# The last tile's gates made in the pass before its own and kept in DRAM (hybrid MLA / sparse attention / PEER step)

## The chip, the cores and the metric

One core of one Trainium2 chip. The time is that of one launch on the device in microseconds (us), from the program's start to its end. The kernel before was run three times: 1798.29 us in the median, 1796.89 and 1798.40 at the ends.

## What is computed

One step of a streaming encoder layer for 512 prompt rows, 32 sample rows and 16 meta rows of 1024 columns, all in float32. Cut to what this case touches:

```
h = RMSNorm(x)
cq, ckv, kpe, bq, bk, bv, iq, iw, ik, ga, gb = split(h @ w_in)
o_a = latent attention(cq, ckv, kpe);  o_b = sparse attention(bq, bk, bv; top keys by iq, iw, ik)
x = x + (sigmoid(ga) * (o_a @ w_o_a) + sigmoid(gb) * (o_b @ w_o_b)) @ w_out
x = x + PEER(RMSNorm(x))
PEER: per row 8 heads pick 16 of 128^2 experts by product keys; for each expert e
      out += softmax weight * gelu(h . u[e]) * v[e]
```

`ga` and `gb`, the gates, are 1024 columns each, so they need the 1024 x 2048 part of `w_in` that the program calls `in_w_gate`: 16 chunks of 512 KB. The experts' rows are 8 KB each (`u` and `v` together, the tensor `in_peer_uv`).

## The kernel before

**Tiles and columns.** Rows are cut into five tiles: i = 0 is the sample tile of 32 rows, i = 1 to 4 are the prompt tiles of 128 rows. PEER is a stream of 544 columns, `NCOL`: for a group of 32 rows and 4 times 32 of its 128 chosen experts, one column gathers 128 rows of 8 KB (1 MB) by an indirect DMA of GpSimd (POOL), line 1330, into one of `RING` = 9 buffers `rows`. VectorE multiplies and sums them with the rows' own values (`dot`, line 2657; the operand `ps_h` is made per 32 columns by `spread` on TensorE, line 1800), ScalarE turns the result into a weight and a diagonal (lines 2155 to 2164), and TensorE mixes the second half of the gathered rows into `ps_v` (`mix`, line 1820), `LAG` = 3 columns behind. POOL issues the gather of column c once the mix of column c - 9 has freed its buffer (line 1328).

**Passes.** The front of the layer (projection, attention, gates, merge, output, PEER's queries) runs in four passes, `PASSES`. Pass 0 makes tiles 0 and 1 before the stream starts. Passes 1, 2 and 3, the looped passes, make tiles 2, 3 and 4 while the stream works through columns 0 to 127, 128 to 255 and 256 to 383; columns 384 to 543 have no pass beside them. `spread_steps` deals the 117 steps of a pass over its 128 columns by a table of estimated costs, and all engines walk the same table (`ticks_at`), each with its own part of a step. In a pass, x = -4 to 27 is the head: load and norm x, turn it into columns (`turn_x`, `x_columns`, buffer `bufh`), project, norm, turn the heads. Then 48 steps hold the index scores, the latent attention and the choice of keys, with the sparse attention's beginning, and at every 6 of them two gate products (`gate`, line 1559: 8 matmuls each of 128 x 128 weights by 128 rows) and one tanh (`tanh_gates`, line 1993). After them come the blend of the attention outputs with the gates (`blend`, `merged`), the product with `w_out`, and PEER's queries.

**Weights.** SyncE (SP) loads each pass's weights in the fixed order of `loads` through a ring of four buffers `wch` of 512 KB (`load`, line 1230); a load waits until TensorE has used what lay in its buffer. One looped pass loads 13 chunks of `w_row`, `w_uq` and `w_ukv`, 16 of `w_gate`, 8 of `w_o`, 8 of `w_out`, 8 of `peer_wq`. Four gate chunks are already asked for before SP waits for the new rows (`s_norm`) and stores them from `pr`, which is a view of the gates' buffer `sg`.

```
for n in range(WRING):
    load_gate(p, n)
sp.wait_ge(s_norm, p)
```

## Time and profile before

| | |
|---|---|
| median of 3 runs | 1798.29 us |
| the profiled execution | 1796.99 us, its span 1795.2 us |
| busy: TensorE, VectorE, ScalarE, POOL | 1223.4, 1310.8, 579.7, 526.2 us |
| DMA | 696.48 MB, 388 GB/s over the span |
| of it, gathers (queue q0) | 570.53 MB |
| mean granted clock of TensorE | 0.787 |
| loads of `w_gate` through the ring | 60 of 512 KB: 12 for pass 0, 16 for each looped pass |

The profile is one execution. Times count from the start of its span. The first 212 us have no stream; the last 400 have only the stream. A DMA share near 1 means that all 16 DMA engines were busy all the time; it can read 1.01 or 1.02.

### The profile page before, as it was taken

How to read it: one execution, taken by the hardware profiler on the slowest of the kernel's cores; microseconds unless marked ns; L12 is line 12 of the kernel's file. 1: busy time of each engine (PE TensorE's matmuls, PEld its weight loads, DVE VectorE, ACT ScalarE, POOL GpSimd, SP SyncE). 2: the span in 40 equal slices, each digit the busy share in tenths (PEclk: the TensorE clock that was granted, in tenths of full speed). 3: DMA queues.
4: the chain of work that ended last, by engine and by line, in shares of the span. 5: the costliest groups of instructions: out<-in, count | busy, mean ns of one | idle time of the engine just before them, and what ended most of it. 6: DMA issues, size and time to landing. Idle time of an engine off the chain costs nothing.

```text
span 1795.2 us, 26399 instructions
## 1 busy us (share of the span) xinstructions
PE 1223.4 (68%) x9056; PEld 679.3 (38%) x9056; DVE 1310.8 (73%) x3857; ACT 579.7 (32%) x1995; POOL 526.2 (29%) x569
## 2 busy tenths in 40 slices
PE   8989976677867575878877666679867343434343
PEld 3668532344535232444535223356535111111111
DVE  5662696989666676989666768998766878686754
ACT  2331134333423333334323334344423222222222
POOL 0200232333322223332322223232323333333332
PEclk9989889787988696897998697887999555555555
DMA  6238699999999999999999999999999999999997
GB/s 267 74 100 294 250 422 421 422 425 425 424 424 423 417 401 383 420 425 424 425 423 422 423 407 390 426 400 398 422 424 423 427 426 426 425 427 423 427 421 294
DMA packets 119381, 696.48 MB, mean 388 GB/s; under 512 B 17983, under 2 KB 21118, under 8 KB 49102
## 3 DMA queue, kind: packets, MB, share of 16 engines
q0 software_dynamic: 78848, 570.53, 76.0%
q1 hardware_dynamic: 36686, 121.83, 17.5%
q10 hardware_dynamic: 3712, 2.43, 0.4%
q8 instruction: 72, 1.18, 0.2%
q14 instruction: 63, 0.52, 0.1%
HBM read 691.65 MB, written 3.02 MB: 387 GB/s over the span
## 4 chain that ended last, share of the span: by engine, by line
DMA 35%; DVE 25%; PE 25%; issue 6%; ACT 3%; POOL 1%; ACTq 0%; DVEq 0%; SPq 0%; POOLq 0%
DMA rows<-in_peer_uv,index 26%; DVE rows L2657 11%; PE ps_v L1820 5%; DMA wch<-in_w_row 4%; PE ps_f L1559 4%; PE ps_f L1353 2%; PE ps_f L1574 2%; PE ps_h L1800 2%; DMA wch<-in_peer_wq 2%; DVE score L2333 1%; PE ps_f L1477 1%; PE ps_f L1653 1%; DVE best L2332 1%; DMA wch<-in_w_ukv 1%; PE ps_f L1437 1%
## 5 line engine op out<-in xcount | busy, mean ns | idle before, releaser
L2657 DVE CUSTOM_DVE_ANT_0 rows<-rows,ps_h 128x1024 f32<-128x1024 f32 x544 | 658.0, 1220 | 289.1 <-DMA rows<-in_peer_uv,index 236.3
L1330 POOL DMA_INDIRECT rows<-in_peer_uv,index x544 | 516.4, 949 | 1169.4 <-PE ps_v L1820 988.8
L1820 PE MATMUL ps_v<-rows,diag 128*32 128x256 f32 x4352 | 419.1, 500 | 432.0 <-ACT diag L2164 424.8
L1820 PEld LDWEIGHTS ps_v<-rows,diag 128*32 128x32 f32 x4352 | 124.2, 130 | 677.5 <-ACT diag L2164 561.7
L2155 ACT ACTIVATE tan<-arg 128x2 f32<-128x2 f32 x272 | 55.3, 203 | 799.2 <-DVE arg L2667 756.4
L2158 ACT ACTIVATE weight<-tan,lead 128x1 f32<-128x1 f32 x544 | 180.8, 379 | 9.1
L2164 ACT ACTIVATE diag<-sel,weight 128x32 f32<-128x32 f32 x544 | 140.9, 306 | 0.6 <-PE ps_v L1820 0.6
L1559 PEld LDWEIGHTS ps_f<-bufh,wch 128*128 128x128 f32 x768 | 103.7, 214 | 19.9 <-issue 17.8
L1559 PE MATMUL ps_f<-bufh,wch 128*128 128x128 f32 x768 | 109.7, 302 | 0.0
L1353 PE MATMUL ps_f<-wch,bufh 128*128 128x512 f32 (+1 forms) x192 | 81.9, 565 | 27.7 <-DMA wch<-in_w_row 26.7
L1653 PE MATMUL ps_f<-bufh,wch 128*128 128x128 f32 x384 | 52.1, 293 | 12.5 <-DMA wch<-in_peer_wq 12.3
L1353 PEld LDWEIGHTS ps_f<-wch,bufh 128*128 128x128 f32 x192 | 32.8, 203 | 72.0 <-issue 36.1
L1653 PEld LDWEIGHTS ps_f<-bufh,wch 128*128 128x128 f32 x384 | 47.8, 203 | 24.1 <-issue 14.2
L1582 PE MATMUL ps_f<-wch,bufb 128*128 128x512 f32 x96 | 47.1, 625 | 13.1 <-DMA wch<-in_w_out 13.1
L1574 PE MATMUL ps_f<-bufq,wch 128*128 128x128 f32 x384 | 54.4, 300 | 1.2 <-ACT bufq L1986 1.2
L1574 PEld LDWEIGHTS ps_f<-bufq,wch 128*128 128x128 f32 x384 | 49.6, 209 | 12.4 <-issue 9.7
L2666 DVE TENSOR_TENSOR lead<-dots,halfw 128x2 f32<-128x2 f32 x272 | 43.8, 161 | 9.4
L1800 PE MATMUL ps_h<-hrows,rep 32*128 32x512 f32 x68 | 46.2, 812 | 3.2 <-DVE dots L2657 3.2
L2657 DVE DVE_READ_ACCUMULATOR2_ANT dots<- 128x1 f32 x544 | 44.7, 82 | 0.0
L2664 DVE SCALAR_TENSOR_TENSOR cube<-dots 128x2 f32<-128x2 f32 x272 | 42.5, 156 | 0.6
L2667 DVE SCALAR_TENSOR_TENSOR arg<-cube,dots 128x2 f32<-128x2 f32 x272 | 42.0, 154 | 0.0
L1937 ACT COPY probT<-ps_f 128x128 f32<-128x128 f32 (+3 forms) x64 | 26.6, 415 | 41.7 <-PE ps_f L1449 29.5
(398 smaller groups left out, 1682.4 us busy)
## 6 DMA issues: line engine op xcount, KB each, us to landing
wch<-in_w_gate SPq DMA_DIRECT2D x60, 512.0 KB
wch<-in_w_row SPq DMA_DIRECT2D x36, 512.0 KB
wch<-in_w_o SPq DMA_DIRECT2D x32, 512.0 KB
wch<-in_w_out SPq DMA_DIRECT2D x24, 512.0 KB
wch<-in_peer_wq SPq DMA_DIRECT2D x24, 512.0 KB
rows<-in_peer_uv,index POOLq DMA_INDIRECT x544
w_tok<-in_w_tok SPq DMA_DIRECT2D x4, 1640.0 KB, 12.9
wch<-in_w_uq SPq DMA_DIRECT2D x6, 384.0 KB
```

The lines of the kernel that those rows point to most:

```text
L1330: pool.indirect_dma_start(rows[c % RING][:, :, :].rearrange("p a d -> p (a d)"), None, io.peer_uv[:, :], at).then_inc(s_uv[c % RING], 16)
L1353: ins = nc.tensor.matmul(ps_f[:, 2 + c % 2, 0:cols], buf_h[:, k, :], w[:, b, :], start=(k == 0), stop=(k == DC - 1))
L1559: ins = nc.tensor.matmul(gated(p)[:, a, :], w[:, k, :], h_of(p)[:, k, 0:n], start=(k == 0), stop=(k == DC - 1))
L1574: ins = nc.tensor.matmul(blended(p, j)[:, x, :], w[:, x, k, :], ot_of(p)[:, x, k, 0:n], start=(k == 0), stop=(k == 3))
L1582: ins = nc.tensor.matmul(ps_f[:, c, :], mt_of(p)[:, k, :], w[:, 512 * c:512 * (c + 1)], start=(k == 0), stop=(k == DC - 1))
L1653: ins = nc.tensor.matmul(ps_f[:, 2 + n % 2, 0:x], w[:, k, :], h_of(p)[:, k, 0:x], start=(k == 0), stop=(k == DC - 1))
L1800: ins = nc.tensor.matmul(ps_h[:, 512 * j:512 * (j + 1)], rep[here, :, :].rearrange("p a m -> p (a m)"), hrows[i % 2][here, 512 * j:512 * ( ...
L1820: ins = nc.tensor.matmul(ps_v[GROUP * a:GROUP * (a + 1), :], diag[:, c % DRING, :], rows[c % RING][:, 1, QD * a:QD * (a + 1)], start=False ...
L2155: nc.scalar.activation(tan[:, s:s + 2], arg[:, s:s + 2], ACT.Tanh, scale=TANH).then_inc(s_tan, 1)
L2158: nc.scalar.activation(weight[:, s + j:s + j + 1], tan[:, s + j:s + j + 1], ACT.Identity, scale=lead[:, s + j:s + j + 1], bias=lead[:, s + ...
L2164: nc.scalar.activation(diag[:, (c + j) % DRING, :], sel[:, :], ACT.Copy, scale=weight[:, s + j:s + j + 1]).then_inc(s_diag, 1)
L2657: v.tensor_tensor_reduce(out=u, in0=u, in1=ps_h[:, :], scale=1.0, scalar=0.0, op0=ALU.mult, op1=ALU.add, accum_out=dots[:, c % KEEP:c % KE ...
```

## The change

Pass 2 (`BOTH`) takes the x rows of the last tile too. SP loads them into `junk` at the pass's start; in the head's first steps, x = -4 to 0, which held nothing, VectorE, ScalarE and TensorE norm and turn them a second time for this tile, into `h_pair[:, 1]`, which lies where `hrows1` lies; `h_pair[:, 0]` is the old `bufh`. Each of the 128 gate matmuls of pass 2 then takes 256 rows in place of 128. The tanh becomes two: one for the pass's own tile into `sg`, one for the last tile into a quarter of `qh`, from where ScalarE's queue stores 128 KB to a DRAM tensor `kept`, eight times. Pass 3 makes no gates and loads no `w_gate`. Once its new rows are stored and `pr` is free, SP loads the 1 MB of `kept` into `sg`, and the loads of `w_o` follow at once. x of the last tile is still loaded and normed in pass 3 for its own projection. Nothing else moves: the table of steps still counts gates in every pass.

```diff
+BOTH = 2
+ASIDE = 4
...
+    at_h = pl.at
...
+    apart = (pl.at - 4 * D - at_h) // 4
+    m.h_pair = Plan(nc, at_h)("hpair", [P, 2 * apart])[:, :].rearrange("p (t s) -> p t s", t=2)
...
     def h_of(p):
+        if p == BOTH:
+            return m.h_pair[:, 0, 0:D].rearrange("p (c k) -> p c k", c=DC)
         return buf_h if p else wide_h
...
-        return few_h if i == 0 else buf_b if i == 1 else buf_h
+        return few_h if i == 0 else buf_b if i == 1 else h_of(i - 1)
...
     def sg_of(p):
+        if p == BOTH + 1:
+            return idle_sg.rearrange("p (j a k) -> p a j k", j=DC, a=2)
         return sg if p else wide_sg
...
+    def gate_width(p):
+
+        return width_of(p) + (P if p == BOTH else 0)
+
+    def gate_rows(p, k):
+
+        return m.h_pair[:, :, P * k:P * (k + 1)] if p == BOTH else h_of(p)[:, k, 0:width_of(p)]
+
+    MORE = PASSES[BOTH][0] - 1
+
+    def turn_of(i):
+
+        return i - 1 + (i > MORE)
+
+    def kept_at(j):
+
+        return qh[:, 2 * (j % ASIDE):2 * (j % ASIDE) + 2, :]
...
     def gated(p):
-        n = width_of(p)
+        n = gate_width(p)
...
     loads = [(p, j) for p in range(NP)
-             for j in (list(range(J_AT, V_AT + 1)) + list(range(K_AT)) if p
+             for j in (list(range(J_AT, V_AT + 1)) + list(range(Z_AT if p == BOTH + 1 else 0, K_AT)) if p
...
     def gates_of(p):
-        return range(0 if p else SOON, DC)
+        return range(DC if p == BOTH + 1 else 0 if p else SOON, DC)
...
+                    if p == BOTH:
+                        sp.wait_ge(s_ot, 2 * (i - 1))
+                        sp.dma_start(junk, io.x_prompt[P * (t + 1):P * (t + 2), :]).then_inc(s_more_x, 16)
                     sp.dma_start(tab, io.tabs[:, t, :]).then_inc(s_tab, 16)
...
-                    for n in range(WRING):
-                        load_gate(p, n)
+                    if p <= BOTH:
+                        for n in range(WRING):
+                            load_gate(p, n)
...
-                for n in range(WRING + (0 if p else 2 * SOON), 2 * DC):
-                    load_gate(p, n)
+                if p == BOTH + 1:
+                    sp.wait_ge(s_pair, 3 * p)
+                    sp.wait_ge(s_qk, p)
+                    sp.wait_ge(s_new, 16 * 5 * p)
+                    for n in range(ASIDE):
+                        sp.wait_ge(s_kept[n], 16 * (DC // ASIDE))
+                    sp.dma_start(idle_sg, m.kept[:, :, :, :].rearrange("p j a k -> p (j a k)")).then_inc(s_back, 16)
+                else:
+                    for n in range(WRING + (0 if p else 2 * SOON), 2 * DC):
+                        load_gate(p, n)
...
-            def turn_x(i):
-                pe.wait_ge(s_xsn, i - 1)
+            def turn_x(i, n):
+                pe.wait_ge(s_xsn, n)
                 pe.wait_ge(s_sc, first_block(i) + 1)
+                if n > 1:
+                    pe.wait_ge(s_ht, 2 * (n - 1))
...
             def gate(p, j, a):
-                n = width_of(p)
                 if a == 0:
...
+                sums = gated(p)[:, a, :]
+                if p == BOTH:
+                    sums = sums.rearrange("p (t k) -> p t k", t=2)
                 for k in range(DC):
-                    ins = nc.tensor.matmul(gated(p)[:, a, :], w[:, k, :], h_of(p)[:, k, 0:n],
-                                           start=(k == 0), stop=(k == DC - 1))
+                    ins = nc.tensor.matmul(sums, w[:, k, :], gate_rows(p, k), start=(k == 0), stop=(k == DC - 1))
...
-                if j == 1:
+                if j == 1 and p <= BOTH:
...
+                        if x == -1 and p == BOTH:
+                            turn_x(i, MORE)
                         if x == 5:
-                            turn_x(i)
+                            turn_x(i, turn_of(i))
...
+                if p == BOTH:
+                    nc.scalar.activation(sg_of(p)[:, :, j, :], gated(p)[:, :, 0:P], ACT.Tanh, scale=0.5)
+                    if j >= ASIDE:
+                        act.wait_ge(s_kept[j % ASIDE], 16 * (j // ASIDE))
+                    nc.scalar.activation(kept_at(j), gated(p)[:, :, P:2 * P], ACT.Tanh, scale=0.5).then_inc(s_sig, 1)
+                    act.wait_ge(s_sig, gates_through(p, j))
+                    act.dma_start(m.kept[:, j, :, :], kept_at(j)).then_inc(s_kept[j % ASIDE], 16)
+                    return
                 nc.scalar.activation(sg_of(p)[:, :, j, 0:width_of(p)], gated(p), ACT.Tanh, scale=0.5).then_inc(s_sig, 1)
...
+                if n == 0 and p == BOTH:
+                    for slot in range(ASIDE):
+                        act.wait_ge(s_kept[slot], 16 * (DC // ASIDE))
                 nc.scalar.copy(qh[:, ASKED[n], :], ps_f[:, 2 + n % 2, 0:P]).then_inc(s_qc, 1)
...
+                        if x == -3 and p == BOTH:
+                            root_x(MORE)
                         if x == 3:
-                            root_x(i)
+                            root_x(turn_of(i))
...
+            def more_sum():
+                dve.wait_ge(s_more_x, 16)
+                x_squares(junk)
+
+            def x_squares(x):
+                step(v.tensor_tensor_reduce(out=sq[:, 0:D], in0=x, in1=x, scale=1.0, scalar=0.0, op0=ALU.mult, op1=ALU.add,
                                             accum_out=px[:, 0:1]), s_step)
...
+            def x_scale(p, x, n):
+                dve.wait_ge(s_rtx, n)
                 for half in range(2):
                     dve.wait_ge(s_key[half], blocks_through(p - 1) + 1)
                 step(v.reciprocal(px[:, 3:4], px[:, 2:3]), s_step)
-                step(v.tensor_scalar(xin, xb[i % 2][:, :], px[:, 3:4], None, ALU.mult), s_xsn)
+                step(v.tensor_scalar(xin, x, px[:, 3:4], None, ALU.mult), s_xsn)
+
+            def more_columns(i):
+                dve.wait_ge(s_h, first_block(i - 1))
+                columns_out(m.h_pair[:, 1, 0:D].rearrange("p (c k) -> p c k", c=DC), MORE)
...
             def merged(p, j):
                 n = width_of(p)
-                if p or j >= SOON:
+                if p == BOTH + 1:
+                    dve.wait_ge(s_back, 16)
+                elif p or j >= SOON:
                     dve.wait_ge(s_sig, gates_through(p, j))
...
+                        if x == -4 and p == BOTH:
+                            more_sum()
+                        if x == -2 and p == BOTH:
+                            x_scale(p, junk, MORE)
+                        if x == 0 and p == BOTH:
+                            more_columns(i)
                         if x == 2:
                             x_sum(i)
                         if x == 4:
-                            x_scale(p, i)
+                            x_scale(p, xb[i % 2][:, :], turn_of(i))
...
+    m.kept = nc.dram_tensor("kept", [P, DC, 2, P], F32).ap()
```

**TensorE's order at the first gates of pass 2.** `ps_v` is the mix of a column, `ps_f` with `bik` an index score, `ps_f` with `bufh` or `hpair` a gate product. Before:

```order
L1437 MATMUL ps_f<-bik,bufb 128x400
L1559 MATMUL ps_f<-bufh,wch_97 128x128 x8
L1820 MATMUL ps_v<-rows_127,diag 32x256 x4
L1820 MATMUL ps_v<-rows_128,diag 32x256 x4
L1437 MATMUL ps_f<-bik,bufb 128x400
L1559 MATMUL ps_f<-bufh,wch_98 128x128 x8
```

Changed:

```order
L1481 MATMUL ps_f<-bik,bufb 128x400
L1605 MATMUL ps_f<-hpair,wch_98 128x256 x8
L1867 MATMUL ps_v<-rows_128,diag 32x256 x4
L1867 MATMUL ps_v<-rows_129,diag 32x256 x4
L1481 MATMUL ps_f<-bik,bufb 128x400
L1605 MATMUL ps_f<-hpair,wch_99 128x256 x8
```

The places are the same (buffer numbers are one higher); each gate matmul is twice as wide.

**SyncE's queue in pass 3**, from the last projection weights on. Before:

```order
L1230 DMA wch_100<-in_w_ukv 128x1024
L1230 DMA wch_97<-in_w_gate 128x1024
L1230 DMA wch_98<-in_w_gate 128x1024
L1230 DMA wch_99<-in_w_gate 128x1024
L1230 DMA wch_100<-in_w_gate 128x1024
L1271 DMA out_new_p<-sg 128x128
L1271 DMA out_new_p<-sg 128x32
L1271 DMA out_new_p<-sg 128x64 x3
L1230 DMA wch_97<-in_w_gate 128x1024
```

Changed:

```order
L1260 DMA wch_101<-in_w_ukv 128x1024
L1305 DMA out_new_p<-sg 128x128
L1305 DMA out_new_p<-sg 128x32
L1305 DMA out_new_p<-sg 128x64 x3
L1318 DMA sg<-kept 128x2048
L1260 DMA wch_98<-in_w_o 128x1024
```

Sixteen gate loads are gone, one load of 1 MB is in their place, and `w_o` moves up behind it.

**VectorE's order at the start of pass 2**, changed (`oab` is `junk`, the last tile's x; the rows L2739 are dots):

```order
L2275 ISA rel,px<-oab 128x1024
L2275 ISA px 128x1
L2277 TENSOR_SCALAR px<-px 128x1
L2739 ISA rows_129,dots<-rows_129,ps_h 128x1024
...
L2283 RECIPROCAL px<-px 128x1
L2284 TENSOR_SCALAR qh<-oab,px 128x1024
...
L2301 TENSOR_TENSOR hpair<-ps_f,ln_51 128x512 x2
```

The first three, the next two and the last (two instructions) are new; the dots between them stood there before.

## Rows read from the trace of the kernel before

**Rows 1.** The page, what the DMA engines moved, GB/s in 40 equal slices.

```profile
GB/s 267 74 100 294 250 422 421 422 425 425 424 424 423 417 401 383 420 425 424 425 423 422 423 407 390 426 400 398 422 424 423 427 426 426 425 427 423 427 421 294
```

**Rows 2.** The page, DMA queues: packets, MB, share of the 16 engines.

```profile
q0 software_dynamic: 78848, 570.53, 76.0%
...
q10 hardware_dynamic: 3712, 2.43, 0.4%
```

**Rows 3.** Busy time by stretch, granted clock, DMA share, GB/s.

```profile
core 0: us, PE busy (x) PEld busy (x) DVE busy (x) ACT busy (x) POOL busy (x), PEclk, DMA share, GB/s
602.00:723.00 121.00, 76.88 (x453) 33.35 (x446) 89.69 (x263) 41.56 (x125) 35.61 (x38) 0.74 0.98 396
723.00:864.00 141.00, 115.43 (x845) 67.92 (x847) 131.33 (x385) 55.07 (x203) 47.97 (x51) 0.86 1.01 424
864.00:998.00 134.00, 95.64 (x819) 58.07 (x815) 81.52 (x230) 41.98 (x137) 37.45 (x40) 0.88 1.02 423
998.00:1107.00 109.00, 69.50 (x416) 31.07 (x408) 81.08 (x233) 38.74 (x114) 31.89 (x34) 0.78 0.99 405
1107.00:1271.00 164.00, 133.57 (x987) 86.07 (x989) 151.22 (x426) 64.27 (x223) 53.63 (x57) 0.85 1.00 409
1271.00:1390.00 119.00, 90.12 (x811) 55.86 (x807) 76.33 (x219) 40.07 (x128) 35.86 (x38) 0.96 1.02 423
1390.00:1780.00 390.00, 165.14 (x1312) 51.05 (x1304) 279.89 (x808) 101.77 (x394) 144.28 (x155) 0.53 1.01 425
```

**Rows 4.** Waits over the whole span, queue of POOL and VectorE: total, times, longest.

```profile
POOL rows L1330 <- PE ps_v L1820: 988.8, 355, 7.3
...
DVE rows L2657 <- DMA rows<-in_peer_uv,index: 236.3, 189, 2.5
```

**Rows 5.** Waits of VectorE, 723 to 864 us.

```profile
DVE rows L2657 <- DMA rows<-in_peer_uv,index: 3.2, 3, 1.5
...
DVE logit L2353 <- PE ps_f L1437: 0.3, 1, 0.3
```

**Rows 6.** Waits of VectorE, 864 to 998 us.

```profile
DVE rows L2657 <- DMA rows<-in_peer_uv,index: 39.2, 22, 2.5
```

**Rows 7.** Waits of VectorE, 1107 to 1271 us.

```profile
DVE logit L2353 <- PE ps_f L1434: 3.6, 4, 1.8
...
DVE rows L2657 <- DMA rows<-in_peer_uv,index: 3.0, 3, 1.3
```

**Rows 8.** Waits of VectorE, 1271 to 1390 us.

```profile
DVE rows L2657 <- DMA rows<-in_peer_uv,index: 28.2, 19, 2.5
```

**Rows 9.** 0 to 1271 us, line L2657 on VectorE, then L1330 on POOL.

```profile
0.00:1271.00 1271.00, 422.39 (x696) 0.85 0.92 377
...
0.00:1271.00 1271.00, 336.27 (x352) 0.85 0.92 377
```

**Rows 10.** TensorE in order of time, gate matmuls: start, us, ..., count.

```profile
112.97 2.34 PE L1559 MATMUL ps_f<-wideh,wch 128*128 128x160 f32 x16
...
1107.62 2.05 PE L1559 MATMUL ps_f<-bufh,wch 128*128 128x128 f32 x16
```

**Rows 11.** VectorE in order of time, start of the second looped pass.

```profile
601.89 1.22 DVE L2657 CUSTOM_DVE_ANT_0 rows<-rows,ps_h 128x1024 f32<-128x1024 f32 x1 [3.41 <-PE ps_h L1800]
...
614.55 1.27 DVE L2208 CUSTOM_DVE_ANT_0 rel<-xb 128x1024 f32<-128x1024 f32 x1 [2.56 <-DMA xb<-in_x_prompt]
...
618.97 0.75 DVE L2217 TENSOR_SCALAR qh<-xb,px 128x1024 f32<-128x1024 f32 x1
```

**Rows 12.** Groups of VectorE by line, 602 to 723 us: busy, mean ns.

```profile
L2227 DVE TENSOR_TENSOR bufh<-ps_f,ln 128x512 f32<-128x512 f32 x2 | 1.3, 684 | 0.0
```

**Rows 13.** DMA issues of SyncE in order of time.

```profile
570.05 0.43 SPq L1255 DMA_DIRECT2D probT<-in_tabs  x1
...
1063.01 7.98 SPq L1230 DMA_DIRECT2D wch<-in_w_gate  x4
```

**Rows 14.** Groups of ScalarE by line, whole span: busy, mean ns, idle before.

```profile
L1993 ACT ACTIVATE sg<-ps_f 128x256 f32<-128x256 f32 x24 | 9.0, 375 | 13.9 <-PE ps_f L1559 13.9
```

25 lines of the change are left out of this document (14 added, 11 removed).

## The prediction

> **What bounds the kernel now.** I read the page's line of transfer rates first, then the DMA queues, then busy time by stretch, then the waits. The rate stands at 420 to 426 GB/s in most of the 40 slices from the sixth on [rows 1], and in the stretch where only the stream runs the 16 DMA engines are full, share 1.01 at 425 GB/s [rows 3]. Gathers take 76% of the engines' span, 570.53 MB for 544 columns [rows 2], so 1.049 MB each, and at 425 GB/s a column cannot pass in under 2.47 us. The waits say the same from the other side: POOL waits 988.8 us for mixes that free a buffer, and VectorE 236.3 us for gathered rows [rows 4]. So bytes look like time.
>
> They are not so everywhere. Five stretches [rows 3] cover passes 2 and 3. In 723 to 864 us, where pass 2 makes its gates, DMA is full (1.01, 424 GB/s) and VectorE is busy 131.33 of 141 us, yet waits only 3.2 us for rows [rows 5]: the two are level. In 864 to 998 us VectorE waits 39.2 us for rows [rows 6]: DMA alone. In 998 to 1107 us the rate is 405, in 1107 to 1271 us, where pass 3 makes its gates, 409 GB/s with VectorE busy 151.22 of 164 us, 92%, and waiting 3.0 us for rows and 3.6 for scores [rows 7]. Here VectorE leads and DMA keeps up with a little to spare. From 1271 us on VectorE waits for rows again, 28.2 us in 119 [rows 8]. So the change takes bytes out of a stretch where VectorE is the bound and puts others into one where DMA has no room. That is the whole argument.
>
> **What is added in pass 2.** The x tile is 0.524 MB, 1.2 us of DMA time at 424 GB/s. Eight stores of 131 KB make 1.05 MB in runs of 1 KB. The nearest rows are the stores of `y`, also runs of 1 KB from SBUF: queue q10 moved 2.43 MB in 0.4% of 1795.2 us, 7.2 us, so 2.96 us per MB [rows 2], and 3.1 us here. As 864 to 998 us is DMA's alone, what DMA owes by then is paid there: +4.3 us. The bounds are 3.7 us, all at 424 GB/s, and 6, if the 0.4% is rounded down from nearly 0.45 and the stores disturb the gathers as much again as that. The Trainium skill, page "DMA: Bandwidth & Descriptors", section Bandwidth, speaks against this part: it counts transfers near 64 KB as mostly overhead and gives 138 GB/s at 64 KB and 341 at 1 MB. An estimate from its 64 KB figure is 1.05 / 0.138 = 7.6 us for the stores in place of 3.1.
>
> VectorE gets the second norm: 1.27 + 0.75 [rows 11] and 2 x 0.68 us [rows 12], with its small operations (some 0.4 us) 3.8 us. It falls where VectorE stood 3.41 us for `ps_h` and then 2.56 us for x [rows 11]; the new sum runs inside the first wait, the new columns before the second, and the later steps find their x landed. I take 0; the bound is 3.8. If that cover were gone, DMA would still run on while VectorE is late, as long as the ring is not full. The x load is issued with the table's, at 570.05 us [rows 13], 30 us before its use, also hidden. Both wait in SP's queue for `s_ot` of tile 2, long past by then, and delay nothing behind them.
>
> TensorE's gate pairs (16 matmuls) take 2.05 us with 128 rows and 2.34 with 160 [rows 10], both at the full clock. In proportion to the second, 256 rows take 3.74; with its slope (0.009 us per row) 3.21; with double the first 4.10. I take 3.74, the value by the widest measured form: 8 x 1.69 = +13.5 us of TensorE (9.3 to 16.4) in 141 us, of which it is busy 115.43 [rows 3]. That fits. VectorE waited 0.3 us for scores there [rows 5], so each gate, 0.85 us longer, mostly lies inside the lead that scores have. I take 0 for the end time, since being late by a few us in 723 to 864 us only moves the wait of 39.2 us behind it. ScalarE issues eight tanhs more, 0.375 us at most each [rows 14], and eight stores: under 7 us, on an engine busy 55.07 of 141 us [rows 3].
>
> **What is removed and added in pass 3.** Sixteen loads, 8.39 MB, 19.8 us of DMA time; 1.05 MB comes back in one load, 2.5 us, beside VectorE's work. TensorE loses 128 matmuls, 8 x 2.05 = 16.4 us. Four of these loads were issued from 1063.01 us [rows 13], the others follow the gates. How much can become time? First, in 1107 to 1271 us, VectorE's waits, 3.0 for rows and 3.6 for scores that queue behind gates [rows 7], and what belongs to them: between 0 and 7.4 us. I take 4.0: the rows' wait goes whole, of the scores' a third. Second, a head start. At 1271 us 352 gathers are issued and 696 / 2 = 348 dots begun [rows 9]: four are under way or landed. When VectorE leaves its stretch with all of them landed instead of just one, it has three columns, 7.4 us, in hand that DMA need not repeat; between 0 and 7.4. Since the rate of 409 says that the ring is already full at times, I take half, 3.7. The rest of the 19.8 us becomes idle DMA: POOL cannot issue further than nine buffers.
>
> **Sum.** +4.3 - 4.0 - 3.7 = -3.4 us. The execution of the profile took 1796.99 us, 1.3 below the median of 1798.29; against the median this is **1794.9 us**.
>
> **The rivals.** About 3.6 us, 0.2%, is what a measurement of this kernel can tell from no change.
>
> *Every byte counts.* If DMA were the bound throughout, the balance is -8.39 + 1.05 + 1.05 + 0.52 = -5.77 MB, in time -19.8 + 2.5 + 3.1 + 1.2 = -13.0 us: 1785.3. For it: the share of 1.00 even in the gates' stretch of pass 3 [rows 3]. Against: all idle time of VectorE there is 12.8 us, most of it not a wait for rows. The Trainium skill, page "Perfetto Trace Analysis", section Identifying the Most-Contended Engine, would have us relieve the most occupied one, which here is DMA, and points at this time; the trace disagrees for the stretch in which the bytes go. Chance 0.13.
>
> *The bytes go where nobody waits.* The ring is already as full as it gets at 1271 us and the scores' wait stays, since it hangs on VectorE's own logits; then pass 3 gives back nothing and pass 2 costs 4.3 us: 1802.6. It decides from the point where the head start and the waits saved come to less than 4.3 us. For it: 92% of VectorE, 3.0 us of waits for rows. Against: DMA showed a full share in that stretch, so the ring cannot be full all the time. Chance 0.22.
>
> *TensorE holds pass 2.* If all 13.5 us fell on VectorE's path, DMA would owe 4.3 of them anyway and the ring covers three columns, 7.4; 1.8 us remain, so -3.4 + 1.8: 1796.7. For it: TensorE is busy 82% there; against: 0.3 us of waits. Chance 0.08.
>
> *The small stores cost as the page has it*, 4.5 us more: 1799.4. Against: the `y` stores, four times smaller, do not. Chance 0.07.
>
> **Numbers.** The forecast's own case has 0.50, and by its bounds (both gains whole, or a third of each) reaches from 1788 to 1800: 0.22 of it over 3.6 us faster, 0.28 within. Every byte: 0.13 faster. Nobody waits: 0.17 slower, 0.05 within. TensorE: 0.03 within, 0.05 slower, since the clock can fall too. Small stores: 0.05 within, 0.02 slower. Together 0.35, 0.41, 0.24. The range that leaves out a tenth on each side runs from 1787, near the every-byte case, to 1803, just over the case without a gain.
>
> **What would show it.** Right: 16 loads of `w_gate` fewer, 690.7 MB; 864 to 998 us begins some 4 us later; the stretch of pass 3's gates is at most 5 us shorter, VectorE above 93% in it, its waits for rows gone and the rate down to about 365 GB/s; the wait of 28.2 us behind it shorter by a few us. The gate pairs of pass 2 take 3.2 to 4.1 us. Wrong: if the gates' stretch of pass 3 shrinks by 10 us or more, VectorE was not its bound. If waits for scores appear in pass 2, TensorE was mis-sized. If the start of pass 2 is late by more than 2 us at x's columns, the second norm was not covered.

## The result, and the profile after

The changed kernel takes 1818.67 us (median of 4 runs, 1816.4 to 1820.87), the kernel before beside it 1797.59 (4 runs, 1795.6 to 1798.4): ratio 1.0117, 95% interval 1.01 to 1.0134. That is 21 us slower. The forecast was 1794.9 with a range up to 1803, so sign and range both missed. The profiled execution took 1816.40 us, its span 1814.6.

The bytes went as written. The page of the kernel after, GB/s in 40 slices, and the DMA queues:

```profile
GB/s 265 85 87 290 299 424 408 405 424 426 424 423 422 392 407 383 401 416 387 392 423 422 424 416 390 402 344 323 377 419 424 413 427 426 426 427 427 427 426 303
DMA packets 118515, 690.68 MB, mean 381 GB/s; under 512 B 17887, under 2 KB 22046, under 8 KB 48110
...
q10 hardware_dynamic: 4864, 3.48, 0.6%
```

690.68 MB are left; the slices with 344, 323 and 377 GB/s (1179 to 1315 us) lie where the kernel before still loaded pass 3's gate weights, and just behind, at 400, 398 and 422 GB/s [rows 1]. To see where the time came from, both kernels are cut at the same work. Every gathered column has one dot on VectorE (L2657 before, L2739 after), 544 in all; the stretches run from the start of one dot to that of another: columns 128 to 168 (head of pass 2), 168 to 216 (its gates), 216 to 256, 256 to 288 (head of pass 3), 288 to 344 (its gates), 344 to 384, and 384 to 543. Busy time by stretch, before:

```profile
core 0: us, PE busy (x) PEld busy (x) DVE busy (x) ACT busy (x) POOL busy (x), PEclk, DMA share, GB/s
601.89:728.21 126.32, 82.20 (x487) 37.12 (x488) 94.76 (x279) 43.36 (x131) 36.47 (x39) 0.74 0.98 398
728.21:861.95 133.74, 108.17 (x792) 62.36 (x792) 124.82 (x363) 52.87 (x195) 46.80 (x50) 0.86 1.01 424
861.95:997.50 135.55, 97.19 (x831) 59.69 (x835) 82.55 (x235) 42.39 (x138) 37.77 (x41) 0.88 1.02 423
997.50:1104.22 106.72, 67.35 (x398) 30.03 (x402) 78.80 (x229) 38.13 (x113) 30.54 (x32) 0.77 0.99 407
1104.22:1262.12 157.90, 127.34 (x936) 80.58 (x934) 147.32 (x413) 60.07 (x207) 52.17 (x56) 0.85 1.00 407
1262.12:1389.84 127.72, 98.84 (x879) 62.59 (x879) 82.85 (x238) 44.88 (x146) 38.51 (x41) 0.96 1.02 424
1389.84:1786.74 396.90, 167.23 (x1328) 51.72 (x1327) 282.84 (x816) 103.85 (x403) 144.44 (x155) 0.53 1.00 419
```

The same seven stretches after:

```profile
601.26:731.29 130.03, 81.41 (x476) 37.92 (x477) 96.79 (x284) 44.63 (x132) 35.76 (x38) 0.76 0.97 393
731.29:879.08 147.79, 129.80 (x796) 78.50 (x794) 124.94 (x364) 53.92 (x198) 45.40 (x49) 0.91 0.99 393
879.08:1012.61 133.53, 101.01 (x849) 62.05 (x851) 82.46 (x237) 43.63 (x143) 40.44 (x42) 0.89 1.02 422
1012.61:1118.68 106.07, 66.54 (x398) 29.84 (x402) 78.64 (x229) 38.14 (x113) 30.88 (x32) 0.79 1.00 406
1118.68:1281.22 162.54, 123.96 (x711) 61.57 (x710) 147.19 (x411) 57.63 (x200) 52.35 (x56) 0.65 0.94 367
1281.22:1412.38 131.16, 103.91 (x851) 63.29 (x847) 82.68 (x238) 44.53 (x145) 37.93 (x41) 0.88 0.99 404
1412.38:1806.01 393.63, 168.68 (x1328) 52.06 (x1327) 282.52 (x815) 103.85 (x403) 144.72 (x155) 0.52 1.00 420
```

Differences in order: +3.7, **+14.1**, -2.0, -0.7, **+4.6**, **+3.4**, -3.3; together +19.9 us. VectorE's busy time is the same in each stretch but for the 2 us of the second norm. In pass 2's gates DMA is no longer full, 0.99 and 393 GB/s for 1.01 and 424, and TensorE is busy 129.80 of 147.79 us. In pass 3's gates VectorE is busy for 91% of a longer stretch, not above 93% of a shorter one. The strangest line is the fifth: TensorE runs 225 instructions fewer, and its busy time falls by 3.4 us only, while its granted clock (PEclk, as a share of full speed) went from 0.85 to 0.65; it is a mean over two levels, 1.2 and 2.4 GHz.

What the gates cost on TensorE is told by their groups over the whole span (busy us, mean ns). Before:

```profile
L1559 PE MATMUL ps_f<-bufh,wch 128*128 128x128 f32 x768 | 109.7, 302 | 0.0
```

After, the wide ones of pass 2, and one entry in order of time:

```profile
L1605 PE MATMUL ps_f<-hpair,wch 128*128 128x256 f32 x256 | 66.4, 418 | 0.0
```

```profile
733.84 3.72 PE L1605 MATMUL ps_f<-hpair,wch 128*128 128x256 f32 x16
```

768 records in three passes are 256 in each: eight matmuls for each of 16 weight chunks, and two records for each matmul. So an entry of 16 records is one chunk, not two, and a pass has 16 such entries. Its gates took 109.7 / 3 = 36.6 us and the wide ones take 66.4, **+29.8 us** where the prediction has +13.5. (Pass 2's own 256 records took 35.2 us before; against them it is +31.2.)

VectorE's waits after, in pass 2's gates (731.29 to 879.08 us), to be held against [rows 5]:

```profile
DVE logit L2427 <- PE ps_f L1481: 9.2, 4, 3.7
DVE score L2393 <- ACT rel L1962: 6.4, 4, 2.3
DVE rows L2739 <- PE ps_h L1847: 2.8, 1, 2.8
```

In pass 3's gates, before (1104.22 to 1262.12 us) and after (1118.68 to 1281.22 us):

```profile
DVE rows L2657 <- PE ps_h L1800: 5.0, 1, 5.0
DVE logit L2353 <- PE ps_f L1434: 2.8, 3, 1.8
```

```profile
DVE rows L2739 <- PE ps_h L1847: 8.1, 2, 4.5
DVE logit L2427 <- PE ps_f L1478: 4.5, 3, 3.0
```

These two waits, both for TensorE, grew by 4.8 us, and the stretch by 4.6. The stretch behind, after (1281.22 to 1412.38 us), against [rows 8]:

```profile
DVE rows L2739 <- DMA rows<-in_peer_uv,index: 18.3, 11, 2.5
DVE inv L2435 <- PE ps_f L1506: 6.2, 1, 6.2
DVE xb L2507 <- PE ps_f L1627: 5.9, 1, 5.9
```

In pass 2 no wait for gathered rows is left; all of them are for scores, `rel` and the token rows, made by TensorE and what hangs on it. Behind pass 3's gates the wait for rows did get shorter, 18.3 us for 29.3 over the same columns, and waits for TensorE took the room (for `inv` 6.2 us for 2.6, for `xb` 5.9 for 3.6).

### The profile page after: what moved, and what is told of

It is laid out like the page before. It is cut to its first block, busy times and chain, and to the rows that moved or that the text cites. A ratio compares the mean times of both kernels' runs of the same rounds, so it can differ in the third digit from the quotient of the medians.

```text
span 1814.6 us, 25907 instructions
## 1 busy us (share of the span) xinstructions
PE 1247.0 (69%) x8808; PEld 679.0 (37%) x8808; DVE 1313.3 (72%) x3864; ACT 582.2 (32%) x1998; POOL 527.1 (29%) x569
## 2 busy tenths in 40 slices
DMA packets 118515, 690.68 MB, mean 381 GB/s; under 512 B 17887, under 2 KB 22046, under 8 KB 48110
## 3 DMA queue, kind: packets, MB, share of 16 engines
q1 hardware_dynamic: 34670, 115.01, 16.4%
## 4 chain that ended last, share of the span: by engine, by line
DMA 34%; PE 27%; DVE 25%; issue 5%; ACT 4%; POOL 1%; ACTq 0%; DVEq 0%; POOLq 0%
DMA rows<-in_peer_uv,index 23%; DVE rows L2739 10%; PE ps_v L1867 6%; PE ps_f L1605 5%; DMA wch<-in_w_row 4%; PE ps_f L1521 2%; PE ps_f L1397 2%; PE ps_h L1847 1%; PE ps_f L1481 1%; DMA wch<-in_w_out 1%; PE ps_f L1619 1%; DMA wch<-in_peer_wq 1%; DVE score L2407 1%; PE ps_f L1627 1%; PE ps_f L1698 1%
## 5 line engine op out<-in xcount | busy, mean ns | idle before, releaser
L2739 DVE CUSTOM_DVE_ANT_0 rows<-rows,ps_h 128x1024 f32<-128x1024 f32 x544 | 656.7, 1220 | 269.5 <-DMA rows<-in_peer_uv,index 213.9
L1867 PE MATMUL ps_v<-rows,diag 128*32 128x256 f32 x4352 | 425.8, 508 | 424.7 <-ACT diag L2224 424.4
L2224 ACT ACTIVATE diag<-sel,weight 128x32 f32<-128x32 f32 x544 | 140.9, 305 | 1.2 <-PE ps_v L1867 1.2
L1397 PE MATMUL ps_f<-wch,bufh 128*128 128x512 f32 (+1 forms) x128 | 55.0, 568 | 18.4 <-DMA wch<-in_w_row 18.3
L1605 PE MATMUL ps_f<-hpair,wch 128*128 128x256 f32 x256 | 66.4, 418 | 0.0
L1605 PEld LDWEIGHTS ps_f<-hpair,wch 128*128 128x128 f32 x256 | 53.3, 212 | 17.9 <-issue 9.1
L2739 DVE DVE_READ_ACCUMULATOR2_ANT dots<- 128x1 f32 x544 | 44.7, 82 | 0.0
L1698 PE MATMUL ps_f<-bufh,wch 128*128 128x128 f32 x256 | 33.9, 288 | 9.2 <-DMA wch<-in_peer_wq 9.1
L1397 PEld LDWEIGHTS ps_f<-wch,bufh 128*128 128x128 f32 x128 | 21.9, 203 | 48.5 <-issue 24.6
L1481 PE MATMUL ps_f<-bik,bufb 64*128 64x144 f32 (+2 forms) x96 | 38.2, 484 | 1.9 <-ACT kt L1954 1.1
## 6 DMA issues: line engine op xcount, KB each, us to landing
wch<-in_w_row SPq DMA_DIRECT2D x36, 512.0 KB, 11.5
wch<-in_peer_wq SPq DMA_DIRECT2D x24, 512.0 KB, 12.3
```

The source lines that it names most:

```text
L1397: ins = nc.tensor.matmul(ps_f[:, 2 + c % 2, 0:cols], h_of(p)[:, k, :], w[:, b, :], start=(k == 0), stop=(k == DC - 1))
L1481: ins = nc.tensor.matmul(ps_f[0:q, u % 2, 0:nk], left, right, start=True, stop=True)
L1605: ins = nc.tensor.matmul(sums, w[:, k, :], gate_rows(p, k), start=(k == 0), stop=(k == DC - 1))
L1867: ins = nc.tensor.matmul(ps_v[GROUP * a:GROUP * (a + 1), :], diag[:, c % DRING, :], rows[c % RING][:, 1, QD * a:QD * (a + 1)], start=False ...
L2224: nc.scalar.activation(diag[:, (c + j) % DRING, :], sel[:, :], ACT.Copy, scale=weight[:, s + j:s + j + 1]).then_inc(s_diag, 1)
L2739: v.tensor_tensor_reduce(out=u, in0=u, in1=ps_h[:, :], scale=1.0, scalar=0.0, op0=ALU.mult, op1=ALU.add, accum_out=dots[:, c % KEEP:c % KE ...
```

## The experiments

Fifteen kernels ran. Ratios are to the kernel before beside each (medians 1796.98 to 1798.83 us); the columns behind are the six stretches of the profiled execution in us, by the columns they cover. Prices below are differences of these ratios, times 1797 us.

| kernel | median us | ratio, 95% interval | 128-168 | 168-216 | 216-256 | 256-288 | 288-344 | 344-384 |
|---|---|---|---|---|---|---|---|---|
| before | 1797.59 | 1 | 126.3 | 133.7 | 135.5 | 106.7 | 157.9 | 127.7 |
| after | 1818.67 | 1.0117, 1.01 to 1.0134 | 130.0 | 147.8 | 133.5 | 106.1 | 162.5 | 131.2 |
| narrow | 1809.00 | 1.0058, 1.004 to 1.0075 | 133.1 | 136.4 | 136.2 | 107.4 | 159.8 | 132.7 |
| no_store | 1813.73 | 1.0107, 1.0076 to 1.0137 | 130.4 | 143.3 | 133.1 | 106.6 | 162.7 | 130.6 |
| tanh_only | 1818.79 | 1.0117, 1.0091 to 1.0143 | 132.5 | 143.0 | 133.0 | 108.4 | 160.0 | 131.2 |
| no_norm | 1811.41 | 1.0086, 1.0067 to 1.0105 | 128.2 | 148.0 | 133.9 | 108.0 | 162.5 | 126.4 |
| warm | 1811.73 | 1.0083, 1.0059 to 1.0107 | 131.9 | 147.7 | 133.8 | 105.2 | 158.1 | 127.5 |
| undone | 1795.17 | 0.998, 0.9966 to 0.9995 | 124.9 | 134.6 | 135.6 | 105.7 | 158.3 | 127.8 |
| no_load | 1793.14 | 0.9982, 0.9965 to 0.9999 | 125.7 | 133.9 | 135.9 | 104.8 | 156.5 | 127.6 |
| few_mm | 1813.14 | 1.0083, 1.0059 to 1.0107 | 125.9 | 134.0 | 135.8 | 107.1 | 163.8 | 129.9 |
| twice | 1807.22 | 1.0049, 1.0033 to 1.0065 | 127.6 | 144.0 | 134.4 | 104.9 | 158.1 | 130.1 |
| warm_head | 1808.18 | 1.0066, 1.0039 to 1.0094 | 130.0 | 134.8 | 135.7 | 109.9 | 157.1 | 130.6 |
| respread_warm | 1815.74 | 1.009, 1.0063 to 1.0118 | 129.9 | 140.9 | 133.7 | 107.0 | 167.4 | 128.5 |
| respread2_warm | 1801.88 | 1.0018, 1.0003 to 1.0033 | 131.3 | 140.6 | 134.2 | 106.7 | 157.9 | 127.9 |
| counted_warm | 1802.36 | 1.0015, 1.0001 to 1.0028 | 127.4 | 141.2 | 131.5 | 107.2 | 156.1 | 126.5 |
| spread3_warm | 1816.02 | 1.0089, 1.0068 to 1.011 | 137.8 | 133.5 | 138.8 | 107.6 | 159.4 | 131.5 |
| before_spread | 1801.44 | 1.001, 0.9995 to 1.0024 | 126.5 | 137.9 | 133.4 | 107.3 | 157.1 | 128.2 |

One profiled execution is one sample, and the table says how far to trust a stretch. Columns 288 to 344 took 156.1 to 159.4 us in the ten kernels in which TensorE has its full work there in its old places, and 159.8 to 163.8 in the six in which it has less: the two sets do not meet, and their means lie 4.2 us apart. Columns 128 to 168 took 124.9 to 128.2 us in the seven without the second norm and without idle matmuls there, and 129.9 to 133.1 in the seven with the norm at its first place, 4.9 us apart. Columns 344 to 384 separate nothing: 126.5 to 131.5 us in the first ten, 126.4 to 132.7 in the six.

### Pass 2: the wide matmuls

The theory after the two traces was that the wider matmuls hold up the scores. (The 13 us of added TensorE time in the expectation below is the prediction's, still miscounted; it is some 30.) The rivals were ScalarE (second tanh, issue of the stores) and the stores themselves. **narrow**, on the changed kernel:

```diff
-        return m.h_pair[:, :, P * k:P * (k + 1)] if p == BOTH else h_of(p)[:, k, 0:width_of(p)]
+        return h_of(p)[:, k, 0:width_of(p)]
...
-                    sums = sums.rearrange("p (t k) -> p t k", t=2)
+                    sums = sums[:, 0:P]
```

> The changed kernel, but the gates' matmuls of pass 2 take only the 128 rows of the pass's own tile again, 2.05 us for 16 as in before, not 3.65. The second tanh, the eight stores and the 1 MB load of pass 3 stay; the gates of the last tile are not computed (left-over sums stand in their place). Theory T (the wider matmuls: TensorE does 13 us more in a stretch in which the scores of the next column are made, and the scores come late): pass 2's gates' stretch falls from 147.8 us back to 134 to 136, the waits of VectorE for logit sums go from 9.2 us to under 1, and the kernel takes 1804 to 1808 us. Theory S (ScalarE holds the stretch: the second tanh, and the issue of the stores and its waits): it stays at 1816 to 1820. Theory D (the stores beside full DMA engines): the same, 1816 to 1820.

**twice** is the opposite edit, on the kernel before:

```diff
-        n = width_of(p)
+        n = width_of(p) + (P if p == 2 else 0)
...
+                    rows_k = mid(buf_h[:, k, :], 2) if p == 2 else h_of(p)[:, k, 0:n]
```

> The kernel before, but the gates' matmuls of pass 2 take 256 rows, the same 128 twice; the output is unchanged. Nothing else of the change is in it: no second tanh, no stores, no second norm, pass 3 as it was. Theory T (wider matmuls in the steps of pass 2 hold the scores up): its gates' stretch grows from 133.7 us by 9 to 12, 11.4 being what narrowing them gave back in the changed kernel, and the kernel takes 1806 to 1810 us. If the wait of 39.2 us for rows behind it absorbs the delay, as the prediction has it: 1797 to 1799 us, with the next stretch shorter by as much.

Taking the width away gives 0.0059 of the ratio back, 10.6 us, and 11.4 us in the stretch; adding it to the kernel before costs 0.0049, 8.8 us, and 10.3 in the stretch. The stretches came as the theory had them, narrow's to 0.4 us; its 1809.0 us is 1 above the forecast. VectorE's waits in pass 2's gates, narrow and then twice:

```profile
DVE rows L2739 <- DMA rows<-in_peer_uv,index: 3.8, 5, 1.5
DVE logit L2427 <- PE ps_f L1481: 1.1, 1, 1.1
DVE score L2393 <- ACT rel L1962: 0.6, 1, 0.6
```

```profile
DVE logit L2357 <- PE ps_f L1437: 9.5, 4, 3.7
DVE score L2323 <- ACT rel L1919: 4.7, 4, 1.6
```

So both waits come and go with the width alone, the one for ScalarE's `rel` too, for in twice ScalarE does nothing that it did not do before. The wait of 39.2 us for rows behind it [rows 6] gave 1.1 us back in twice (135.5 to 134.4), not 10. VectorE's waits of that stretch in twice (875.17 to 1009.61 us):

```profile
DVE rows L2661 <- DMA rows<-in_peer_uv,index: 33.6, 20, 2.5
DVE inv L2365 <- PE ps_f L1462: 6.9, 1, 6.9
```

Before, over the same columns, they are 39.6 us for rows and 2.2 for `inv`. The wait for rows did shrink, by 6.0 us, and 4.7 of them came back as a wait for TensorE. The rates say why DMA could not lend more: in the gates' stretch of twice it moved 401 GB/s for 144.03 us, 57.8 MB, for 56.7 before, so in 10.3 us more it got only about 1 MB, one column of 2.5 us, ahead. That it stopped there for want of a free buffer, of which the ring has nine, is argued and was not tried by itself.

**no_store** takes the second tanh and the stores out of the changed kernel, **tanh_only** the stores and the waits for them alone (of the lines below all but the one with the tanh); in both the 1 MB of pass 3 comes from the gate weights:

```diff
-                    if j >= ASIDE:
-                        act.wait_ge(s_kept[j % ASIDE], 16 * (j // ASIDE))
-                    nc.scalar.activation(kept_at(j), gated(p)[:, :, P:2 * P], ACT.Tanh, scale=0.5).then_inc(s_sig, 1)
-                    act.wait_ge(s_sig, gates_through(p, j))
-                    act.dma_start(m.kept[:, j, :, :], kept_at(j)).then_inc(s_kept[j % ASIDE], 16)
```

> The changed kernel with its wide matmuls, but without the second tanh and without the eight stores of pass 2; pass 3 loads 1 MB from the gate weights in place of the kept gates, so the output rests on other numbers there. Theory T (wider matmuls on TensorE): 1816 to 1820 us, with pass 2's gates' stretch within 2 us of 147.8. Theory S (second tanh and waits of ScalarE) or D (stores): 1804 to 1808 us, and the stretch at 134 to 137.

> The changed kernel with the second tanh of pass 2, but without the eight stores and their waits; pass 3's 1 MB comes from the gate weights. Against the run without both (stretch of pass 2's gates 143.3 us, median 1813.7) it tells the tanh from the stores. If ScalarE's second tanh is the cost (the wide gates' buffer is released later): the stretch is 146 to 148 us. If the stores and their waits in ScalarE's queue are: 142 to 144 us. As pass 3 is unchanged, 1811 to 1818 us in both cases; the stretch decides.

The stretch went to 143.3 us without both and to 143.0 without the stores, so what counts there is the stores and their waits in ScalarE's queue, 4.5 to 4.8 us, and the tanh is hidden. That is neither theory of no_store, which had all or nothing. The three kernels with wide gates and stores there (after, no_norm, warm) have 147.7 to 148.0 us, the three with wide gates and no stores (these two and twice) 143.0 to 144.0; where the gates are narrow the stores add less, 136.4 in narrow for 133.7 to 134.8 without. The medians tell less: 1.0107 and 1.0117 lie within each other's interval and beside after's, so in the whole time the stores cost 0 to 5 us.

### Pass 3: the clock

**warm** adds idle work to the changed kernel, and nothing waits for it:

```diff
+                    if p == BOTH + 1 and 0 <= k < 6 * DC and k % 6 in (2, 4):
+                        for c in range(DC):
+                            nc.tensor.matmul(ps_f[:, 3, 0:P], h_of(p)[:, c, :], h_of(p)[:, c, :],
+                                             start=(c == 0), stop=(c == DC - 1))
```

> The changed kernel, with eight matmuls of 128 rows on TensorE added at each of the 16 places of pass 3 where before had its gates' matmuls; their sums go to an unused part of a PSUM bank, nothing waits for them and nothing is loaded for them. Theory C (in pass 3 TensorE does less without the gates, its granted clock falls from 0.85 to 0.65, and the scores and turns take longer by more than VectorE gains): the granted clock of 1119 to 1281 us returns to 0.80 or more, the stretch of pass 3's gates falls from 162.5 us to 152 to 157, the next one from 131.2 to 127 to 129, and the kernel takes 1808 to 1813 us. Theory O (pass 3 is longer for another reason, the order of the work or the 1 MB load, and the clock only goes with it): 1818 to 1822 us, no gain from more work.

**few_mm** takes work out of the kernel before:

```diff
-                for k in range(DC):
+                for k in (0, DC - 1) if p == 3 else range(DC):
```

> The kernel before with all its loads, but pass 3's gates are made by two of their eight matmuls each, so the gates of the last tile are part sums. TensorE loses 96 matmuls of 128 rows there, DMA nothing. Theory C (the clock of pass 3 follows what TensorE does, and the scores follow the clock): the granted clock of 1107 to 1271 us falls from 0.85 to under 0.72, the gates' stretch of pass 3 grows from 157.9 us by 2 to 6 and the next from 127.7 by 2 to 4, so 1801 to 1807 us from less work. Rival O (the clock does not matter, fewer matmuls only help): 1793 to 1798 us.

Busy time by stretch for columns 288 to 344 and 344 to 384, warm, then few_mm:

```profile
1120.73:1278.84 158.11, 127.90 (x936) 81.42 (x936) 147.25 (x413) 57.98 (x200) 52.71 (x56) 0.83 0.95 373
1278.84:1406.32 127.48, 99.70 (x879) 62.27 (x879) 82.63 (x239) 44.34 (x145) 39.31 (x41) 0.95 1.01 423
```

```profile
1105.93:1269.73 163.80, 126.21 (x769) 68.74 (x769) 147.35 (x412) 60.46 (x208) 52.45 (x56) 0.70 0.97 392
1269.73:1399.64 129.91, 102.27 (x851) 62.91 (x853) 83.19 (x236) 44.47 (x144) 38.81 (x41) 0.90 1.01 421
```

More work is faster and less work slower. The clocks came as forecast; warm's stretch of the gates, 158.1 us, stayed 1 above its range, and few_mm's median is 6 above its own. With 128 idle matmuls (256 records, 37.0 us of TensorE) the clock is back at 0.83, the two stretches are 8.1 us shorter together, and the ratio falls by 0.0034, 6.1 us. With 96 matmuls fewer and every byte still loaded, the clock falls to 0.70, the stretches grow by 8.1 us, and the kernel loses 0.0083, 15 us; its eight runs spread from 1803.28 to 1818 us, and the profiled one, at 1805.69, shows only 8.7 of the 15. The spread goes with the clock: the three runs with a mean granted clock of 0.764 to 0.766 took 1803 to 1806 us, the five with 0.745 to 0.756 took 1810 to 1818. Of the 8.1 us in either trace only the part in the gates' stretch, 4.4 and 5.9, is clear of what columns 344 to 384 do by themselves. Where the time of the gates went is seen in TensorE's groups of columns 288 to 344: the same 448 mixes, and the scores, in before, after, warm and few_mm:

```profile
L1820 PE MATMUL ps_v<-rows,diag 128*32 128x256 f32 x448 | 39.1, 439 | 25.1 <-ACT diag L2164 24.4 <-issue 0.8
L1559 PE MATMUL ps_f<-bufh,wch 128*128 128x128 f32 x224 | 31.9, 302 | 0.0
L1434 PE MATMUL ps_f<-bik,bufb 64*128 64x264 f32 x57 | 18.6, 449 | 0.4
```

```profile
L1867 PE MATMUL ps_v<-rows,diag 128*32 128x256 f32 x448 | 49.3, 541 | 33.9 <-ACT diag L2224 33.9
L1478 PE MATMUL ps_f<-bik,bufb 64*128 64x264 f32 x56 | 24.4, 575 | 0.1
```

```profile
L1871 PE MATMUL ps_v<-rows,diag 128*32 128x256 f32 x448 | 38.9, 442 | 24.9 <-ACT diag L2228 24.9
```

```profile
L1820 PE MATMUL ps_v<-rows,diag 128*32 128x256 f32 x448 | 45.4, 505 | 33.3 <-ACT diag L2164 33.3
```

After, 31.9 us of gates are gone, 10.2 us more go to the same mixes and 5.8 to the same scores, and busy falls by 3.4 in all. VectorE's waits for `ps_h` and logits there, 7.8 us before and 12.6 after, are 7.6 in warm and 12.3 in few_mm: so the slower matmuls reach the end. The Trainium skill, page "TensorE: Matmul & The Clock Gate", section What's actually happening, says that the clock is gated by how busy the array has been of late; the granted clocks of 0.85, 0.65, 0.83 and 0.70 agree.

**no_load** is the saving alone: the kernel before without pass 3's 16 loads, its matmuls fed with the tile's own rows as weights:

```diff
...
-                w = use(p, G_AT + 2 * j + a)[:, :].rearrange("p (c k) -> p c k", c=DC)
+                w = buf_h if p == 3 else use(p, G_AT + 2 * j + a)[:, :].rearrange("p (c k) -> p c k", c=DC)
```

> The kernel before without the 16 loads of gate weights in pass 3 (8.39 MB), its gates' matmuls kept there and fed with the tile's own rows as weights, so the gates of the last tile are other numbers. It has the saving of the change at its price of nothing: no wide matmuls, no stores, and TensorE as busy as before. The prediction's terms for the bytes (4.0 us of waits in pass 3 and 3.7 us of head start for the ring of gathers) give 1788 to 1791 us, with a granted clock of 0.83 to 0.87 in 1107 to 1271 us. If all bytes count: 1784 to 1786 us. If the bytes are taken out where nobody waits for them: 1796 to 1799 us. If the loads that went were themselves what held the clock up: the clock falls below 0.75 and the time is over 1800 us.

0.9982 is 3.2 us faster, between the forecast's 7.7 and nothing. (Its profiled execution, 1787.12 us, is the fastest of its ten, whose median is 1793.14.) The clock stayed at 0.85, so the fall in the changed kernel comes from the matmuls, not from the loads.

### The head of pass 2

**no_norm** leaves out the second norm (x load, sum, root, scale, transposes, columns) and feeds the wide matmuls the own rows twice.

> The changed kernel without the second norm at the head of pass 2: no second x load, sum, root, scale, eight transposes and two column writes. The wide matmuls of the gates take the pass's own 128 rows twice, so the gates of the last tile rest on the wrong rows. Theory H (the second norm is on VectorE's path at the head, where the prediction took 0 with a bound of 3.8 us): the stretch of columns 128 to 168, 130.0 us after and 126.3 before, falls to 126 to 127, and the time by 3 to 5 us to 1813 to 1816. Rival (the head is longer through what stands ahead of it, by chance of the execution): no change, 1817 to 1820 us. Pass 2's gates' stretch stays at 146 to 148 us in both.

It takes 0.0031 of the ratio off, 5.6 us. The stretch of the head shows 1.8 in this one trace, 4.9 in the means of seven kernels with the norm and seven without; the 4.8 us that columns 344 to 384 are shorter here lie within what these do by themselves. What the head does is seen in order of time. TensorE before and after, 605 to 612 us:

```profile
605.07 1.08 PE L1811 MATMUL ps_v<-xb,ident 128*32 128x256 f32 x8 [0.49 <-ACT yo L2172]
```

```profile
608.23 1.97 PE L1383 MATMUL ps_f<-ident,qh 128*128 128x128 f32 x8 [4.28 <-DVE qh L2284]
610.13 1.08 PE L1858 MATMUL ps_v<-xb,ident 128*32 128x256 f32 x8
```

SyncE's load of the pass's own x, before and after:

```profile
606.21 0.33 SPq L1241 DMA_DIRECT2D xb<-in_x_prompt  x1
```

```profile
611.27 0.33 SPq L1271 DMA_DIRECT2D xb<-in_x_prompt  x1
```

The new transposes (L1383) stand on TensorE ahead of the matmuls that are the last to read `xb` (L1858), and wait 4.28 us there for VectorE's `qh`. Those matmuls free the buffer into which the own x is loaded, so that load starts 5.06 us later, VectorE waits 5.21 us for it in place of 2.56 [rows 11], and its scale comes at 623.45 us, not 618.97. The Trainium skill, page "PSUM — Partial Sum Buffer", section Engine vs sequencer instructions, has it that matmuls start in program order; the trace agrees: L1858 starts at 610.13 us, right behind L1383, and shows no wait of its own. Most of the price is thus a wait in the wrong place, not the 3.8 us of work: counted_warm, below, does the same work in another order and has 127.4 us there.

### Is it placement? The table of steps

Steps are spread over the columns by the costs in `step_work`, which counts the wide gates of pass 2 like narrow ones and pass 3's as if they were still there. **respread_warm**, with warm's idle matmuls:

```diff
-        if 0 <= k < 6 * DC and k % 6 in (2, 4):
-            pe += DC * small
+        if 0 <= k < 6 * DC and k % 6 in (2, 4) and p < 3:
+            pe += DC * small * (1.8 if p == 2 else 1)
```

> The changed kernel with two edits: the table that sets at which column each step stands counts pass 2's gates at 1.8 times their cost and pass 3's at none, and pass 3 has the eight idle matmuls of 128 rows at each of the 16 places where its gates stood. If the loss in pass 2 is that steps stand too close together for the wider matmuls, its gates' stretch falls from 147.8 us to 138 to 143 and what follows grows by less; with the clock's 6 us of the run before: 1803 to 1809 us. If TensorE is short of time over the whole pass, spreading moves the loss only: 1810 to 1814 us, as with the idle matmuls alone.

The time, 1815.74 us, missed both forecasts. Pass 2's gates gained 6.8 us against warm, 147.7 to 140.9, and pass 3's lost 9.3, 158.1 to 167.4: their steps drew together while the idle matmuls stood between them. That half of the edit was my mistake, and **respread2_warm** drops it (no `p < 3`).

> The changed kernel with the idle matmuls in pass 3, and the table counts pass 2's gates at 1.8 times their cost; unlike the run before, pass 3's steps stay where they are. Pass 2's gates' stretch is at 140 to 142 us as there, not 147.7, pass 3's at 157 to 159, not 167.4. Then 1804 to 1808 us: the crowding of the wide steps is about half of their price, TensorE's added time itself the other half. If the room gained in the gates' stretch is lost behind it, 1810 to 1813 us.

1.0018, 11.7 us less than warm and 2 below the forecast: the largest step back of all, for one factor in a table. The stretch of pass 2's gates shows 7.1 of it, the six stretches together 5.7; their two profiled executions are 3.4 us apart, so the size is the runs', the place the trace's. **counted_warm** also enters the second norm:

```diff
+    if p == 2:
+        pe_head[-1] = DC * small
+        dve_head.update({-4: 2.9, -2: 2.3, 0: 2.9})
```

> As the run of 1801.9 us (gates of pass 2 at 1.8 times, idle matmuls in pass 3), and the table also counts the second norm at the head of pass 2: VectorE's three steps and TensorE's eight transposes. If the norm's price (126 to 130 or 131 us for columns 128 to 168) is crowding: that stretch at 127 to 129 us and 1798 to 1801 us in all. If it is a chain of waits that more room only stretches: 131 to 135 us and 1802 to 1806 us.

The head is at 127.4 us, and here the freeing matmuls (now L1866) stand ahead of the transposes (L1387) again:

```profile
607.49 1.08 PE L1866 MATMUL ps_v<-xb,ident 128*32 128x256 f32 x8 [1.97 <-ACT yo L2240]
...
612.42 1.97 PE L1387 MATMUL ps_f<-ident,qh 128*128 128x128 f32 x8
```

The load of x is issued at 608.63 us and VectorE does not wait for it. Its six stretches sum to 789.8 us against 798.6 in respread2_warm, but the medians, 1.0015 and 1.0018, do not differ; the profiled execution, 1797.5 us, was one of its faster ones. The stretches show the mechanism, the whole time shows no gain, where 1798 to 1801 us were expected.

**before_spread** puts the 1.8 into the kernel before, **spread3_warm** a 3 in its place into respread2_warm.

> The kernel before, of which only the table counts pass 2's gates at 1.8 times their cost, with the matmuls as narrow as they were. If the gain of the respread (7.1 us in pass 2's gates' stretch of the changed kernel) belongs to the wide matmuls: no gain here, 1797 to 1801 us, the stretch at 134 to 137 us. If it is a better table in general: 1790 to 1794 us, the stretch at 127 to 131.

> The changed kernel with pass 3's idle matmuls, as in the run of 1801.9 us, but pass 2's gates counted at 3 times their cost, not 1.8. If crowding is all of the wide matmuls' price, their stretch falls further from 140.6 us to 135 to 138 and the time to 1797 to 1800 us. If TensorE's added time is what is left, or the later steps now crowd: 140 to 145 us there, or more in the next stretch, 1802 to 1808 us.

The factor does nothing for narrow gates (1.001, with 1 inside the interval; their stretch even grows by 4.1 us and the next gives 2.2 back), so it is no better table in general. At 3 the gates' stretch comes down to 133.5 us, that of the kernel before, and the head in front pays 6.5 and the stretch behind 4.6 us of it back: 1.0089, 1816.0 us where at most 1808 was expected. So the wide matmuls' price is partly crowding: 1.8 took 7 us off their stretch and 3 no more from the whole. That what is left is TensorE's own time, which can only be moved, is the reading that fits, and is not shown by itself.

### Two controls

**undone** takes all four additions out of the changed kernel at once (narrow, no norm, no tanh and stores, idle matmuls in pass 3).

> The changed kernel with all four additions taken out at once: pass 2's gate matmuls narrow, no second norm, no second tanh and stores, and the idle matmuls of 128 rows in pass 3. The gates of the last tile are not computed; of the change only the missing 8.39 MB of loads, the missing waits for them and the one 1 MB load stay. If the separate prices are the whole account (wide matmuls 9 to 11 us, clock 6 to 8, norm 3 to 6, tanh and stores 2 to 5), it ends where the kernel before without the loads did: 1791 to 1796 us, with the stretches at 126, 134, 157 and 128 us. If something else of the change costs (the wait ahead of pass 3's load, the shared buffer, the order), it stays over 1799 us.

0.998, the same as no_load's 0.9982. The separate prices against after's 1.0117 are 0.0059 for the width, 0.0034 for the clock, 0.0031 for the norm and 0.0010 for tanh and stores, 0.0134 in all; undone shows 0.0137. The account closes, within what the intervals allow: each price is a difference of two ratios and good to some 0.0025 to 0.0035, 4 to 6 us. By the whole time alone the width is clear of nothing, clock and norm barely, tanh and stores not; width and clock are each shown from both sides, and all four in the stretches.

**warm_head** tried idle matmuls in the kernel before, around 600 to 630 and 990 to 1020 us, where the clock stood at 0.50:

```diff
+                        if -9 < x < 5 and p >= 2:
+                            for c in range(DC):
+                                nc.tensor.matmul(ps_f[:, 3, 0:P], ident[:, :], ident[:, :], start=(c == 0), stop=(c == DC - 1))
```

> The kernel before with eight idle 128-row matmuls of TensorE at each of 13 early steps of the heads of passes 2 and 3, where the granted clock stood at 0.50 (590 to 630 and 980 to 1020 us) and the mixes of a column took 1.93 us for 16 matmuls instead of 1.07. Theory C, taken further (a head is on the path and a higher clock shortens it): the stretches of columns 128 to 168 and 256 to 288, 126.3 and 106.7 us, each get 1 to 4 us shorter, 1790 to 1795 us. Rival (the heads wait for gathered rows, DMA is full there, and idle matmuls only stand in the way): 1797 to 1802 us.

A miss: the clock rose from 0.74 to 0.80 and 0.77 to 0.89 in the two heads, and both got longer, 126.3 to 130.0 and 106.7 to 109.9 us. Its x load is issued late, and VectorE waits for it:

```profile
617.61 0.33 SPq L1241 DMA_DIRECT2D xb<-in_x_prompt  x1
```

```profile
DVE rel L2211 <- DMA xb<-in_x_prompt: 10.1, 1, 10.1
```

It is the same chain as in the changed kernel's head: the matmuls that free `xb` start at 616.91 us behind blocks of idle ones at 606.08, 610.59 and 613.14, where before they started at 605.07. In pass 3's head VectorE waits 11.5 us for x in place of 3.2. A higher clock alone did not shorten a head. Of the versions that compute everything, none beats the kernel before; no_load and undone do by 0.2%, and both leave the right gates of the last tile unmade.

## Why the prediction was wrong

**Pass 2, TensorE (took 0, measured 10.6 us).** The step that failed first is a count: "8 x 1.69 = +13.5 us". The time of an entry was right, 3.62 to 3.72 us at the full clock where 3.74 was forecast; but I read its 16 records as 16 matmuls, a pair of chunks, and they are one chunk of eight matmuls with two records each. There are 16 entries, so the term is 16 x 1.69 = 27 us by the forecast's own price, and 30 to 31 by the trace. With 115.43 us busy that makes 142 of 141 us: "That fits" was wrong on rows that were already read, since a group with its count would have said 256 in place of 128. The next step, "I take 0 for the end time, since being late [...] only moves the wait of 39.2 us behind it", failed too: twice got 1.1 us back there of 10.3, since 4.7 of the 6.0 us that the wait for rows lost became a wait for TensorE. The rival *TensorE holds pass 2* named the mechanism, with the halved size and a credit of 4.3 + 7.4 us for DMA's debt and the ring, and so came to 1.8 us and a chance of 0.08.

**Pass 3, the clock (not in the sum, measured 6.1 us).** "TensorE loses 128 matmuls, 8 x 2.05 = 16.4 us" has the same halving, 32.8 is right, and was written down as neither gain nor loss. The trace of before had the warning: granted clocks of 0.85 and 0.96 in these stretches, and 0.53 where TensorE is busy 165 of 390 us [rows 3]. Taking work from an engine whose clock follows its work makes the rest of the work slower, and TensorE's score, turn and mix matmuls were in the chain.

**The second norm (took 0, bound 3.8; measured 5.6 in the ratio, 4.9 in the head over seven kernels with and without it).** I looked at VectorE's 2.56 us wait for x and called it cover. It was a link of a chain: the load's start hung on TensorE matmuls behind which I had not looked for the new transposes. The prediction's own check, x's columns late by more than 2 us, came out at 4.5.

**The stores (3.1 us forecast).** The stretch shows 4.5 to 4.8 us, the ratio 0 to 5. q10 rose from 0.4% to 0.6% of the engines' time; its packets took 10.7 us of the 16 engines in place of 7.8, so the forecast of their DMA time was right (2.9 us). The 1.2 us for the x load were not taken apart. Whether the stretch pays for that or for ScalarE's waits at them stays open.

**The bytes of pass 3 (-7.7 us forecast).** no_load gives -3.2, undone -3.6, with the 1 MB load. The mechanism held: the rate fell to 367 GB/s, in no_load to 375 (365 forecast), and in no_load the stretches of pass 3 give 1.4 and 0.1 us, that of its head 1.9. The waits saved, put at 4.0, gave 1.4. The head start, put at 3.7, is not in the stretch behind; the last one, columns 384 to 543, is 4.2 us shorter in no_load (392.75 for 396.90), but twice and warm_head, which load everything, have 394.25 and 393.35, so hardly any of it is the loads'.

With these terms +10.6, +6.1, +5.6, +1.8 (tanh and stores) and -3.4 make 20.7 us, where 21 were measured. That it is so close is more than the terms, good to 4 to 6 us each, can promise.

## What to carry to other kernels

Take the size of an edit from a group with its count, not from one entry times a number of your own, and ask whose result stands behind the added work in the engine's program order. Before work is taken from TensorE, look at its granted clock and at who waits for the matmuls that stay. And where steps are laid out by a table of costs, a change of a step's cost is not made until the table has it: here that factor was worth more than the bytes saved.

## What was not expected

Sixteen blocks of matmuls whose sums nobody reads, 37.0 us of TensorE time, made the changed kernel 6 us faster, and leaving out 96 needed ones made the kernel before 15 us slower. Such idle matmuls at the heads of passes cost 12 us; there they stood ahead of a buffer's release. And of the 19.8 us of DMA time that pass 3 no longer needs, 3.2 us reached the end: DMA was 100% busy in that stretch before, at 407 GB/s, and was still not what bounded it.
